# Modulation units moved between the halves of a weight split, spread over more phases, and combined in five parts

## The chip, the cores and the metric

The kernel runs on one core of a Trainium2 chip. The metric is the device time of one execution in microseconds (us). The engines are TensorE (PE, matrix products), VectorE (DVE), ScalarE (ACT), GpSimd (POOL) and SyncE (SP, which issues most of the DMA transfers). Each works through its own instructions in order and waits for semaphores that the others raise.

## The reference: two pairs of layers on 256 tokens of width 1024

The first block has two layers, each a token mixer (latent attention with twelve heads, then sliding-window attention with ALiBi and sinks), cross attention to 256 memory rows, an output projection, and a squared-relu MLP of width 4096. The second block has an even layer (short convolution and a gated linear recurrence) and an odd layer (stick-breaking attention with 16 heads), each with a SwiGLU network of width 2816. Its two layers are modulated by a vector c:

```python
def ada_modulation(c, ada_w, ada_b):
    m = jax.nn.silu(c) @ ada_w + ada_b
    return jnp.split(m, N_MOD, axis=-1)
...
    sh_m, sc_m, g_m, sh_f, sc_f, g_f = ada_modulation(c, ada_w, ada_b)
    h = modulate(rms_norm(x, mix_norm), sh_m, sc_m)
...
    x = x + g_m[:, None, :] * y
    hf = modulate(rms_norm(x, ffn_norm), sh_f, sc_f)
    return x + g_f[:, None, :] * swiglu(hf, ffn_w_gate, ffn_w_up, ffn_w_down)
```

ada_w is 1024 x 6144 per layer, c a single row of 1024. So per layer six vectors of 1024 numbers are needed: shift, scale and gate of the mixer, and the same of the network. The product does not depend on x; it can be worked out any time before the second block wants it.

## The kernel before

**The weight stream.** All large weights pass through rings of two slots of 2 MB each, in the order w_in, mem0, w_uq, w_ukv, mem1, w_o0 (2 slots), up0 (8), down0 (8), swa (4), w_o1 (2), up1 (8), down1 (8), lru_in (5), lru_out (2), gate_up0 (11), ffn_down0 (8), qkv (6), sb_out (2), gate_up1 (11), ffn_down1 (8). Products are made of two numbers of reduced precision per value. SP loads a slot into raw in two transfers; ScalarE's split (L738) copies it to w_hi in two halves, for which it waits until TensorE is through with the slot two before; VectorE's split (L1255) makes w_lo = raw - w_hi, also in two halves, each as soon as that half of w_hi is there. TensorE's two_bank_slot (L2234) waits for both halves of w_lo and then does 2 banks x 2 blocks x 8 chunks x 3 products = 96 matmuls of 256 columns (L2172 to L2174). A slot of ffn_down has 66.

**What stands around a split on VectorE.** In an up slot, hidden (L1812) makes a_lo of bank 0 and of bank 1 (L1819), each after ScalarE has taken that bank (relu and square, L1007 to L1012), and then the split of the slot after next. In a down slot there is only the split, with add_to_residual at j=3. In gate_up, hidden (L2029) multiplies gate by up (L2038), makes a_lo (L2040) and splits. In ffn_down a turn (L2068) is split, add (the product, gated, goes to x, L2053), split.

**The modulation.** The 2 x 6144 outputs are 24 groups of 512 (12 per layer), each of 4 quarters of the 1024 inputs: 96 *units*. A unit needs 512 KB of ada_w, which the POOL queue loads (L571) into one of two buffers; load m waits until unit m - 2 has been worked off. On VectorE a unit is two operations of 128x512 (L1761, the first of a group is L1758). After four units ada_group_done (L1774) transposes the sums (L1779) and reduces them (L1782) into ada_part. When a layer's 12 groups are there, ada_combine on TensorE (L2222) adds the four quadrants with four small matmuls into the norm bank's second half, and modulation on VectorE (L1785) adds the bias and makes the gains.

**Where the units stand before.** Always two at a time, by phase: w_o0 4 units, up0 16, down0 16, swa 4, w_o1 4, up1 16, down1 16, gate_up0 20. In up they stand between the two a_lo of a slot, in down ahead of the split, in gate_up0 ahead of the multiply, in w_o behind the add (the second pair), in swa behind the split. So every unit stands ahead of the split of its slot or behind it, never inside. Layer 0's combination is in the middle of up1 (behind four slots), layer 1's in ffn_down0 behind its first turn. The loops over slots are hardware loops on VectorE in mlp, gate_up and ffn_down.

## Time and profile before

| | us |
|---|---|
| median of three runs | 1190.78 (1190.17 to 1193.43) |
| the profiled execution | 1182.13 |
| its span | 1180.5 |
| TensorE busy | 1156.9 (98%) |
| VectorE busy | 881.7 (75%) |
| ScalarE busy | 634.3 (54%) |
| granted TensorE clock, mean | 1.00 of full speed |

Times in the views count from the start of the span. In a row of the timeline, what stands in brackets is how long the engine was idle before the row and which instruction of which engine released it; "x4" is a run of four instructions of one kind, and the duration is that of the run.

### The profile page before, as it was taken

What the parts mean: (1) busy time and instruction counts of PE and PEld (TensorE: products, weight loads), DVE (VectorE), ACT (ScalarE), POOL (GpSimd) and SP (SyncE); (2) the same over time, 40 slices, a digit from 0 to 9 for tenths busy, and PEclk for the clock granted to TensorE, in tenths of its full rate; (3) what the DMA queues carried; (4) which work ended last, traced back from release to release, by engine and by line L of the source; (5) the groups of instructions that cost most, each with busy time, mean ns of one, the idle gap of its engine ahead of it and who ended that gap; (6) DMA issues with size and microseconds to landing.
All of it is one profiled execution on the core that took longest, in us unless ns stands there. A gap on an engine that the chain in (4) does not pass through costs nothing.

```text
span 1180.5 us, 23101 instructions
## 1 busy us (share of the span) xinstructions
PE 1156.9 (98%) x9525; PEld 1119.7 (95%) x9525; DVE 881.7 (75%) x1174; ACT 634.3 (54%) x853; POOL 95.6 (8%) x147
## 2 busy tenths in 40 slices
PE   8999999999989999999999999999999999999998
PEld 8999999999988999999999999999988879999998
DVE  5876898878876798888998888887576557855543
ACT  7558566633347567634468463443455574634332
POOL 0000011111124011111200001010000000000000
PEclk9999999999999999999999999999999999999999
DMA  9352588887772488788844657877645504565462
GB/s 329 138 179 73 190 292 272 312 308 235 263 267 72 157 275 305 273 302 294 306 167 143 198 159 253 281 265 240 207 165 172 199 1 143 186 206 180 146 196 85
DMA packets 150060, 248.97 MB, mean 211 GB/s; under 512 B 5553, under 2 KB 80922, under 8 KB 149978
## 3 DMA queue, kind: packets, MB, share of 16 engines
q1 hardware_dynamic: 135858, 197.17, 49.6%
q0 software_dynamic: 13952, 50.60, 11.8%
q8 instruction: 60, 0.98, 0.4%
q14 instruction: 22, 0.18, 0.0%
q10 hardware_dynamic: 168, 0.04, 0.0%
HBM read 246.74 MB, written 1.05 MB: 210 GB/s over the span
## 4 chain that ended last, share of the span: by engine, by line
PE 67%; DVE 17%; ACT 4%; issue 3%; DMA 3%; POOL 0%; DVEq 0%; POOLq 0%; ACTq 0%
PE ps L2172 19%; PE ps L2173 19%; PE ps L2174 19%; DVE w_lo L1260 7%; DVE scratch L1761 4%; DMA ada_raw<-in_l_ada_w 3%; ACT w_hi L745 2%; PE ps L2454 2%; PE ps L2320 1%; PE ps L2764 1%; PE ps L2436 1%; DVE ps L1779 1%; ACT h_both L812 1%; PE ps L2738 1%; PE ps L2423 1%
## 5 line engine op out<-in xcount | busy, mean ns | idle before, releaser
L1260 DVE TENSOR_TENSOR w_lo<-raw,w_hi 128x2048 fp32r<-128x2048 f32 (+4 forms) x196 | 412.7, 2144 | 88.4 <-ACT w_hi L745 87.9
L745 ACT ACTIVATE w_hi<-raw 128x2048 fp32r<-128x2048 f32 (+4 forms) x196 | 342.2, 1791 | 156.4 <-PE ps L2174 151.9
L2172 PE MATMUL ps<-h_both,w_hi 128*128 128x256 f32 (+1 forms) x1296 | 360.6, 278 | 7.9 <-DVE w_lo L1260 4.4
L2173 PE MATMUL ps<-h_both,w_hi 128*128 128x256 f32 (+1 forms) x1296 | 358.8, 277 | 0.0
L2174 PE MATMUL ps<-h_both,w_lo 128*128 128x256 f32 (+1 forms) x1296 | 358.7, 277 | 0.0
L2172 PEld LDWEIGHTS ps<-h_both,w_hi 128*128 128x128 f32 (+1 forms) x1296 | 242.7, 187 | 9.9 <-issue 5.0
L2173 PEld LDWEIGHTS ps<-h_both,w_hi 128*128 128x128 f32 (+1 forms) x1296 | 243.4, 188 | 0.1
L2174 PEld LDWEIGHTS ps<-h_both,w_lo 128*128 128x128 f32 (+1 forms) x1296 | 242.7, 187 | 0.0
L2172 PE MATMUL ps<-a_both,w_hi 128*128 128x256 f32 x864 | 238.8, 276 | 0.6 <-DVE xT L2053 0.6
L2173 PE MATMUL ps<-a_both,w_hi 128*128 128x256 f32 x864 | 238.5, 276 | 0.0
L2174 PE MATMUL ps<-a_both,w_lo 128*128 128x256 f32 x864 | 238.5, 276 | 0.0
L2172 PEld LDWEIGHTS ps<-a_both,w_hi 128*128 128x128 f32 x864 | 162.2, 188 | 0.8 <-DVE xT L2053 0.8
L2173 PEld LDWEIGHTS ps<-a_both,w_hi 128*128 128x128 f32 x864 | 162.2, 188 | 0.0
L2174 PEld LDWEIGHTS ps<-a_both,w_lo 128*128 128x128 f32 x864 | 162.2, 188 | 0.0
L1761 DVE SCALAR_TENSOR_TENSOR scratch<-ada_raw,silu_c,scratch 128x512 f32<-128x512 f32 x168 | 126.2, 751 | 13.6 <-DMA ada_raw<-in_l_ada_w 6.1
L571 POOL DMA_DIRECT2D ada_raw<-in_l_ada_w x96 | 69.5, 724 | 623.6 <-DVE scratch L1761 623.3
L1153 ACT ACTIVATE a_both<-a_full 128x512 fp32r<-128x512 f32 x18 | 11.4, 633 | 107.5 <-DVE a_full L2038 107.5
L1007 ACT ACTIVATE a_full<-ps 128x512 f32<-128x512 f32 x32 | 19.0, 595 | 51.2 <-PE ps L2174 51.1
L2172 PE MATMUL ps<-h_wide,w_hi 128*128 128x258 f32 x160 | 45.8, 286 | 0.2 <-DVE xT L1441 0.2
L2173 PE MATMUL ps<-h_wide,w_hi 128*128 128x258 f32 x160 | 45.4, 284 | 0.0
L2174 PE MATMUL ps<-h_wide,w_lo 128*128 128x258 f32 x160 | 45.3, 283 | 0.0
L2172 PE MATMUL ps<-w_hi,h_both 128*128 128x512 f32 (+1 forms) x112 | 42.8, 382 | 0.7 <-issue 0.7
(423 smaller groups left out, 1806.6 us busy)
## 6 DMA issues: line engine op xcount, KB each, us to landing
ada_raw<-in_l_ada_w POOLq DMA_DIRECT2D x96, 512.0 KB, 6.9
raw<-in_mlp_w_up SPq DMA_DIRECT2D x32, 1024.0 KB, 6.4
raw<-in_mlp_w_down SPq DMA_DIRECT2D x32, 1024.0 KB, 6.9
raw<-in_l_ffn_w_gate SPq DMA_DIRECT2D x22, 1024.0 KB, 5.4
raw<-in_l_ffn_w_up SPq DMA_DIRECT2D x22, 1024.0 KB, 8.6
raw<-in_l_ffn_w_down SPq DMA_DIRECT2D x16, 768.0 KB, 6.0
raw<-in_l_w_qkv SPq DMA_DIRECT2D x12, 1024.0 KB, 6.9
raw<-in_l_w_in SPq DMA_DIRECT2D x10, 1024.0 KB, 6.3
```

The lines of the kernel that those rows point to most:

```text
L571: pool.dma_start(ada_raw[:, slot, :, :], ada[l][:, 2 * quarter:2 * quarter + 2, group])\
L745: nc.scalar.activation(w_hi[:, s.slot, cut], raw[:, s.slot, cut], ACT.Copy).then_inc(split_hi, 1)
L812: ins = nc.scalar.activation(h_hi[:, ch, :], xT[:, ch, :], ACT.Copy, scale=col_a[:, gain_at + ch:gain_at + ch + 1])
L1007: nc.scalar.activation(full, acc(b if j else FIRST_UP_BANKS[b]).rearrange("p (c t) -> p c t", c=2), ACT.Relu)\
L1260: nc.vector.tensor_tensor(w_lo[:, s.slot, cut], raw[:, s.slot, cut], w_hi[:, s.slot, cut].bitcast(F32), ALU.subtract).then_inc(split_lo, 1)
L1761: ins = nc.vector.scalar_tensor_tensor(ada_sum, w, c, ada_sum, ALU.mult, ALU.add)
L1779: nc.vector.transpose(ps[:, ADA_BANK, :], ada_sum).then_inc(ada_turned, 1)
L2172: nc.tensor.matmul(to, sh, mh, start=first, stop=False, skip_group_check=True)
L2173: nc.tensor.matmul(to, sh, ml, start=False, stop=False, skip_group_check=True)
L2174: return nc.tensor.matmul(to, sl, mh, start=False, stop=last, skip_group_check=True)
L2320: ins = nc.tensor.transpose(ps[0:ncols, bank, ch * T + t * P:ch * T + (t + 1) * P], src(ch, t), ident[:, :])
L2454: ins = nc.tensor.matmul(ps[:, 6 + g % 2, qt * T + j * HD:qt * T + (j + 1) * HD], p[:, n * P:(n + 1) * P], v, start=j == 0 and n == 0, sto ...
```

## The change

One counter now runs over the units, and a call asks for the next n of them. Where they stand:

- w_o0 2, up0 14 (1, 1 and then 2 per slot), down0 14 (not in its last slot), swa 2, w_o1 2, up1 12 (1, 1, 1, 2, 2, 2, 1, 2), down1 14, gate_up0 18, ffn_down0 6, qkv 4, gate_up1 8.
- In up, down and gate_up they stand between the two halves of the split; in ffn_down0 ahead of a turn's first split; in qkv, w_o and swa behind a split.
- The combination and modulation come in five parts of 8, 4, 6, 4 and 2 groups: behind up1, in lru_in behind slot 1, in ffn_down0 behind the first turn, in sb_out behind slot 0, and ahead of ffn_down1.
- VectorE's loops over slots are written out. POOL issues the same 96 loads, in other portions around its work on masks.

```diff
+MOD_PARTS = ((0, 8, 0), (8, 12, 1), (12, 18, 0), (18, 22, 1), (22, 24, None))
+UP_UNITS = ((1, 1, 2, 2, 2, 2, 2, 2), (1, 1, 1, 2, 2, 2, 1, 2))
...
+            def ada_units(n):
+
+                for m in range(ada_begun[0], ada_begun[0] + n):
+                    ada_unit(m)
+                    if m % 4 == 3:
+                        ada_group_done(m // 4)
+                ada_begun[0] += n
...
+            def modulation(k):
+
+                first, last, which = MOD_PARTS[k]
+                l, at, n = first // ADA_GROUPS, 4 * (first % ADA_GROUPS), 4 * (last - first)
+                c = COL_B[f"ada_b{l}"] + at
+                dve.wait_ge(ada_combined, k + 1)
+                nc.vector.tensor_tensor(mod[:, l, at:at + n], ps[:, NORM_BANK, T:T + n], col_b[:, c:c + n], ALU.add).then_inc(mod_kept, 1)
+                dve.wait_ge(mod_kept, k + 1)
+                if which is not None:
+                    key = ("mix", "ffn")[which] + str(l)
+                    link(nc.vector.scalar_tensor_tensor(modg[:, l, which, :], mod[:, l, 8 + 24 * which:16 + 24 * which], 1.0,
+                                                        col_a[:, COL_A[key]:COL_A[key] + KD], ALU.add, ALU.mult))
...
             split(Slot("w_o0", 1))
-            ada_units("w_o0", 0)
+            ada_units(2)
             add_to_residual("w_o0", 0, following="mlp0")
             split(Slot("w_o0", 2))
             add_to_residual("w_o0", 1, following="mlp0")
-            ada_units("w_o0", 1)
...
+                def hidden(j):
...
+                    split(Slot(f"up{l}", j + 2), (0,))
+                    ada_units(UP_UNITS[l][j])
+                    split(Slot(f"up{l}", j + 2), (1,))
...
-                for j in range(8):
+                for j in range(7):
...
-                    ada_units(f"down{l}", j)
                     following = ("attn1", "final")[l]
                     if j == 3:
                         add_to_residual(f"down{l}", 0, following, pairs=(0,))
-                    if j < 7:
-                        split(Slot(f"down{l}", j + 2))
+                    split(Slot(f"down{l}", j + 2), (0,))
+                    ada_units(2)
+                    split(Slot(f"down{l}", j + 2), (1,))
...
             split(Slot("swa", 3))
-            ada_units("swa", 1)
             wait_part(Slot("swa", 2), 0)
...
-            ada_units("w_o1", 1)
             mlp(1)
...
             split(Slot("lru_in", 3))
+            modulation(1)
...
-                    split(ahead)
+                    split(ahead, (0,))
+                    if j < 10 or l == 0:
+                        ada_units(2 - l)
+                    split(ahead, (1,))
...
+                for i in range(3):
+                    if l == 0:
+                        ada_units(2)
+                    split(Slot(f"ffn_down{l}", 2 * i + 2))
+                    add(i)
+                    split(Slot(f"ffn_down{l}", 2 * i + 3))
+                    if l == 0 and i == 0:
+                        modulation(2)
...
                     split(Slot("qkv", j + 2))
+                if 1 <= j < 5:
+                    ada_units(1)
...
             split(Slot("sb_out", 1))
+            modulation(3)
             add_gated("sb_out", 0, 1, "ffn1")
...
+            def ada_combine(k):
+
+
+                first, last, _ = MOD_PARTS[k]
+                pe.wait_ge(ada_summed, last)
+                if k:
+                    pe.wait_ge(mod_kept, k)
...
             as_chunks_arrive("sb_out", 3)
+            ada_combine(3)
             two_bank_slot("sb_out", 1)
```

How the instructions stand at three places, on VectorE and once on TensorE. (The line numbers of the changed kernel differ a little: its w_lo is L1262, its units L1761 and L1764, its transpose and reduction L1780 and L1782, the gated adds L1466 and L2045, the combining matmuls L2219.)

VectorE in up0, from the split of one slot to the split of the next (a_both is a_lo, the rows of L1761 and L1764 are two units that end a group), before:

```order
L1260 TENSOR_TENSOR w_lo<-raw,w_hi 128x2048 [waits split_hi] x2
L1819 TENSOR_TENSOR a_both<-a_full,a_both 128x512 [waits hid_hi]
L1761 SCALAR_TENSOR_TENSOR scratch<-ada_raw,silu_c,scratch 128x512 [waits ada_step,ada_loaded0]
L1761 SCALAR_TENSOR_TENSOR scratch<-ada_raw,silu_c,scratch 128x512 [waits ada_step]
L1761 SCALAR_TENSOR_TENSOR scratch<-ada_raw,silu_c,scratch 128x512 [waits ada_step,ada_loaded1]
L1761 SCALAR_TENSOR_TENSOR scratch<-ada_raw,silu_c,scratch 128x512 [waits ada_step]
L1779 STREAM_TRANSPOSE ps<-scratch 128x512 [waits ada_step]
L1782 TENSOR_REDUCE ada_part<-ps 128x16 [waits ada_turned]
L1819 TENSOR_TENSOR a_both<-a_full,a_both 128x512 [waits hid_hi]
L1260 TENSOR_TENSOR w_lo<-raw,w_hi 128x2048 [waits split_hi] x2
```

and with the change:

```order
L1262 TENSOR_TENSOR w_lo<-raw,w_hi 128x2048 [waits split_hi]
L1819 TENSOR_TENSOR a_both<-a_full,a_both 128x512 [waits hid_hi] x2
L1262 TENSOR_TENSOR w_lo<-raw,w_hi 128x2048 [waits split_hi]
L1764 SCALAR_TENSOR_TENSOR scratch<-ada_raw,silu_c,scratch 128x512 [waits ada_step,ada_loaded0]
L1764 SCALAR_TENSOR_TENSOR scratch<-ada_raw,silu_c,scratch 128x512 [waits ada_step]
L1764 SCALAR_TENSOR_TENSOR scratch<-ada_raw,silu_c,scratch 128x512 [waits ada_step,ada_loaded1]
L1764 SCALAR_TENSOR_TENSOR scratch<-ada_raw,silu_c,scratch 128x512 [waits ada_step]
L1780 STREAM_TRANSPOSE ps<-scratch 128x512 [waits ada_step]
L1782 TENSOR_REDUCE ada_part<-ps 128x16 [waits ada_turned]
L1262 TENSOR_TENSOR w_lo<-raw,w_hi 128x2048 [waits split_hi]
```

The units, their transpose and reduction stood behind the a_lo of bank 0 and ahead of that of bank 1, and so ahead of the whole split; now they stand behind both a_lo and behind the first half of the split, and only its second half follows them. At the mouth of up0, where a pair and its group's end stood between h_both and the split of slot 1, nothing stands now.

VectorE at the end of gate_up0 and the first turn of ffn_down0, before (a_full and a_both are the multiply and a_lo of the last gate_up slot, the first w_lo is ffn_down0's slot 1, the second its slot 2, xT the add of the turn):

```order
L2038 TENSOR_TENSOR a_full<-a_full,ps 128x512 [waits acc_out0,parts_done]
L2040 TENSOR_TENSOR a_both<-a_full,a_both 128x512 [waits hid_hi]
L1260 TENSOR_TENSOR w_lo<-raw,w_hi 128x1408 [waits split_hi] x2
L1761 SCALAR_TENSOR_TENSOR scratch<-ada_raw,silu_c,scratch 128x512 [waits ada_step,ada_loaded0]
L1761 SCALAR_TENSOR_TENSOR scratch<-ada_raw,silu_c,scratch 128x512 [waits ada_step]
L1761 SCALAR_TENSOR_TENSOR scratch<-ada_raw,silu_c,scratch 128x512 [waits ada_step,ada_loaded1]
L1761 SCALAR_TENSOR_TENSOR scratch<-ada_raw,silu_c,scratch 128x512 [waits ada_step]
L1779 STREAM_TRANSPOSE ps<-scratch 128x512 [waits ada_step]
L1782 TENSOR_REDUCE ada_part<-ps 128x16 [waits ada_turned]
L1260 TENSOR_TENSOR w_lo<-raw,w_hi 128x1408 [waits split_hi] x2
L2053 SCALAR_TENSOR_TENSOR xT<-ps,mod,xT 128x256 [waits parts_done] x2
```

and with the change:

```order
L1764 SCALAR_TENSOR_TENSOR scratch<-ada_raw,silu_c,scratch 128x512 [waits ada_step]
L1764 SCALAR_TENSOR_TENSOR scratch<-ada_raw,silu_c,scratch 128x512 [waits ada_step,ada_loaded1]
L1764 SCALAR_TENSOR_TENSOR scratch<-ada_raw,silu_c,scratch 128x512 [waits ada_step]
L1262 TENSOR_TENSOR w_lo<-raw,w_hi 128x1408 [waits split_hi]
L1764 SCALAR_TENSOR_TENSOR scratch<-ada_raw,silu_c,scratch 128x512 [waits ada_step,ada_loaded0]
L1764 SCALAR_TENSOR_TENSOR scratch<-ada_raw,silu_c,scratch 128x512 [waits ada_step]
L1764 SCALAR_TENSOR_TENSOR scratch<-ada_raw,silu_c,scratch 128x512 [waits ada_step,ada_loaded1]
L1764 SCALAR_TENSOR_TENSOR scratch<-ada_raw,silu_c,scratch 128x512 [waits ada_step]
L1780 STREAM_TRANSPOSE ps<-scratch 128x512 [waits ada_step]
L1782 TENSOR_REDUCE ada_part<-ps 128x16 [waits ada_turned]
L1262 TENSOR_TENSOR w_lo<-raw,w_hi 128x1408 [waits split_hi] x2
L2045 SCALAR_TENSOR_TENSOR xT<-ps,mod,xT 128x256 [waits parts_done] x2
```

Here the first three L1764 rows are of the pair of the last gate_up slot, which now stands inside the split of ffn_down0's slot 1; the next pair follows behind a single half of w_lo, where before a whole split, and with it the wait for w_hi, stood between two pairs.

VectorE at sb_out, before (h_both is the attention's output, xT the gated add of slot 0, bank by bank):

```order
L1747 TENSOR_TENSOR h_both<-ps,h_both 128x512 [waits mix_hi] x2
L1260 TENSOR_TENSOR w_lo<-raw,w_hi 128x2048 [waits split_hi] x2
L1464 SCALAR_TENSOR_TENSOR xT<-ps,mod,xT 128x256 [waits parts_done]
L1464 SCALAR_TENSOR_TENSOR xT<-ps,mod,xT 128x256
L1464 SCALAR_TENSOR_TENSOR xT<-ps,mod,xT 128x256 [waits parts_done]
L1464 SCALAR_TENSOR_TENSOR xT<-ps,mod,xT 128x256
```

and with the change:

```order
L1749 TENSOR_TENSOR h_both<-ps,h_both 128x512 [waits mix_hi] x2
L1262 TENSOR_TENSOR w_lo<-raw,w_hi 128x2048 [waits split_hi] x2
L1791 TENSOR_TENSOR mod<-ps,col_b 128x16 [waits ada_combined]
L1795 SCALAR_TENSOR_TENSOR modg<-mod,col_a 128x8 [waits mod_kept]
L1466 SCALAR_TENSOR_TENSOR xT<-ps,mod,xT 128x256 [waits parts_done,dve_step]
L1466 SCALAR_TENSOR_TENSOR xT<-ps,mod,xT 128x256
L1466 SCALAR_TENSOR_TENSOR xT<-ps,mod,xT 128x256 [waits parts_done]
L1466 SCALAR_TENSOR_TENSOR xT<-ps,mod,xT 128x256
```

The two operations of modulation(3) have come in ahead of the first gated add, with a wait for TensorE's combination. On TensorE that stands between the two slots of sb_out:

```order
L2160 MATMUL ps<-h_both,w_hi 128x256
L2161 MATMUL ps<-h_both,w_lo 128x256
L2219 MATMUL ps<-ada_part,line_h 32x16 [waits mod_kept,ada_summed]
L2219 MATMUL ps<-ada_part,line_h 32x16 x3
L2159 MATMUL ps<-h_both,w_hi 128x256 [waits acc_out0,split_lo]
L2160 MATMUL ps<-h_both,w_hi 128x256
```

The matmul behind it, the first of slot 1, waits for acc_out0, the add of bank 0, and for w_lo.

## Rows read from the trace of the kernel before

**Rows 1.** Page, busy time per engine, and TensorE's granted clock in 40 slices.
```profile
PE 1156.9 (98%) x9525; PEld 1119.7 (95%) x9525; DVE 881.7 (75%) x1174; ACT 634.3 (54%) x853; POOL 95.6 (8%) x147
...
PEclk9999999999999999999999999999999999999999
```

**Rows 2.** TensorE's waits over the whole span: us in total, times, longest.
```profile
PE ps L2172 <- DVE w_lo L1260: 4.4, 3, 2.0
...
PE ps L2422 <- DVE qx L1890: 3.3, 1, 3.3
...
PE ps L2172 <- DVE xT L1441: 1.8, 2, 1.7
```

**Rows 3.** Timeline of VectorE at the mouth of up0: start, us, line, tiles, [idle before].
```profile
142.50 3.18 DVE L1761 SCALAR_TENSOR_TENSOR scratch<-ada_raw,silu_c,scratch 128x512 f32<-128x512 f32 x4
...
147.08 4.48 DVE L1260 TENSOR_TENSOR w_lo<-raw,w_hi 128x2048 fp32r<-128x2048 f32 x2
```

**Rows 4.** Timeline of TensorE, same place.
```profile
151.61 0.39 PE L2172 MATMUL ps<-h_both,w_hi 128*128 128x256 f32 x1 [1.96 <-DVE w_lo L1260]
```

**Rows 5.** Timelines at the head of swa: VectorE, then TensorE.
```profile
343.49 3.22 DVE L1761 SCALAR_TENSOR_TENSOR scratch<-ada_raw,silu_c,scratch 128x512 f32<-128x512 f32 x4 [2.42 <-DMA ada_raw<-in_l_ada_w]
...
350.25 0.34 PE L2422 MATMUL ps<-swa_kT,swa_qT 64*128 64x128 f32 x1 [3.34 <-DVE qx L1890]
```

**Rows 6.** Timeline of ScalarE in up0.
```profile
195.92 0.60 ACT L1007 ACTIVATE a_full<-ps 128x512 f32<-128x512 f32 x1 [3.51 <-PE ps L2174]
...
206.80 0.60 ACT L1007 ACTIVATE a_full<-ps 128x512 f32<-128x512 f32 x1 [3.51 <-PE ps L2174]
```

**Rows 7.** Timeline of VectorE in up0.
```profile
193.83 0.48 DVE L1758 TENSOR_SCALAR scratch<-ada_raw,silu_c 128x512 f32<-128x512 f32 x1
...
199.69 4.49 DVE L1260 TENSOR_TENSOR w_lo<-raw,w_hi 128x2048 fp32r<-128x2048 f32 x2 [0.89 <-ACT w_hi L745]
```

**Rows 8.** Timeline of down0: ScalarE, then VectorE.
```profile
239.50 3.73 ACT L745 ACTIVATE w_hi<-raw 128x2048 fp32r<-128x2048 f32 x2 [5.40 <-PE ps L2174]
...
241.46 4.49 DVE L1260 TENSOR_TENSOR w_lo<-raw,w_hi 128x2048 fp32r<-128x2048 f32 x2 [1.56 <-ACT w_hi L745]
```

**Rows 9.** Timeline of VectorE in gate_up1, slots without units.
```profile
1039.29 0.69 DVE L2038 TENSOR_TENSOR a_full<-a_full,ps 128x512 f32 x1 [3.19 <-PE ps L2174]
...
1042.48 4.50 DVE L1260 TENSOR_TENSOR w_lo<-raw,w_hi 128x2048 fp32r<-128x2048 f32 x2 [1.00 <-ACT w_hi L745]
```

**Rows 10.** Timeline around ffn_down0's first turn: VectorE, then ScalarE.
```profile
804.89 3.16 DVE L1260 TENSOR_TENSOR w_lo<-raw,w_hi 128x1408 fp32r<-128x1408 f32 x2 [0.58 <-ACT w_hi L745]
...
808.56 3.21 DVE L1761 SCALAR_TENSOR_TENSOR scratch<-ada_raw,silu_c,scratch 128x512 f32<-128x512 f32 x4 [0.50 <-DMA ada_raw<-in_l_ada_w]
...
820.46 0.20 DVE L1789 TENSOR_TENSOR mod<-ps,col_b 128x48 f32<-128x48 f32 x1
...
824.58 2.65 ACT L745 ACTIVATE w_hi<-raw 128x1408 fp32r<-128x1408 f32 x2 [5.95 <-PE ps L2174]
...
832.06 1.38 ACT L745 ACTIVATE w_hi<-raw 128x1408 fp32r<-128x1408 f32 x1 [4.83 <-PE ps L2174]
```

**Rows 11.** Line L571, the modulation loads' issues, over the whole span.
```profile
DMA to landing us min/median/max: 4.0/6.9/9.0
```

**Rows 12.** Timeline of TensorE at the first combination, in up1.
```profile
454.60 0.28 PE L2174 MATMUL ps<-h_both,w_lo 128*128 128x256 f32 x1
...
455.09 0.39 PE L2172 MATMUL ps<-h_both,w_hi 128*128 128x256 f32 x1
```

**Rows 13.** Timeline at sb_out: VectorE, then TensorE.
```profile
979.73 0.87 DVE L1464 SCALAR_TENSOR_TENSOR xT<-ps,mod,xT 128x256 f32<-128x256 f32 x2 [2.76 <-PE ps L2174]
...
980.88 0.28 PE L2172 MATMUL ps<-h_both,w_hi 128*128 128x256 f32 x1
```

**Rows 14.** Window behind swa's stop: length, busy us of each engine, PEclk, DMA share, GB/s.
```profile
352.00:366.00 14.00, 13.01 (x111) 11.31 (x109) 7.05 (x28) 10.53 (x35) 9.01 (x6) 1.00 0.01 2
```

**Rows 15.** Timeline of VectorE in qkv, one of four reductions.
```profile
892.23 0.69 DVE L2116 TENSOR_REDUCE sb_ms<-sb_sq 128x8 f32<-128x512 f32 x1 [2.58 <-ACT sb_sq L1186]
```

More of the change, by code:

```diff
@@ L125 @@
 ADA_GROUPS = 12
-ADA_SLOTS = ADA_GROUPS + 1
-ADA_GROUP = {"w_o0": 0, "up0": 1, "down0": 5, "swa": 9, "w_o1": 10, "up1": 11, "down1": 15, "gate_up0": 19}
+MOD_PARTS = ((0, 8, 0), (8, 12, 1), (12, 18, 0), (18, 22, 1), (22, 24, None))
+UP_UNITS = ((1, 1, 2, 2, 2, 2, 2, 2), (1, 1, 1, 2, 2, 2, 1, 2))
 HIDDEN_BEFORE = {"0": 0, "1": 16, "ffn0": 32, "ffn1": 43}
@@ L1750, in _, with ada_unit @@
             ada_sum = scratch[:, 2:4, :].rearrange("p c t -> p (c t)")
-            def ada_unit(m, slot, quarter, loads):
-                dve.wait_ge(ada_loaded[slot], loads)
+            def ada_unit(m):
+                slot, quarter = m % 2, m % 4
+                dve.wait_ge(ada_loaded[slot], 16 * (m // 2 + 1))
                 for q in range(2):
@@ L1762, in ada_unit @@
                     ins.then_inc(ada_step, 1)
-            def ada_units(phase, j, i=None):
-                slot_no = 2 * ADA_GROUP[phase] + j
-                grow = (lambda per, first: first) if i is None else (lambda per, first: i * per + first)
-                for u in range(2):
-                    ada_unit(grow(4, 2 * slot_no + u), u, 2 * (j % 2) + u, grow(32, 16 * (slot_no + 1)))
-                if j % 2:
-                    layer = ADA_GROUP[phase] > ADA_GROUP["w_o1"] if i is not None else slot_no // 2 >= ADA_GROUPS
-                    ada_group_done(grow(1, slot_no // 2 + 1), ADA_SLOTS if layer else 0)
@@ L1785, in modulation @@
[L1785 to L1793 removed]
+            ada_begun = [0]
@@ L1829, in mlp @@
                 link(nc.vector.tensor_tensor(r_squared, r_squared, r_squared, ALU.mult))
-                hidden(1)
-                if l:
-                    dve.wait_ge(ada_combined, 1)
-                with dve.Fori(2, 4) as i:
-                    hidden(i)
-                for j in range(8):
+                for j in range(2, 8):
+                    hidden(j)
+                for j in range(7):
                     if l and j == 1:
@@ L2061, in ffn @@
                 split(Slot(f"gate_up{l}", 3))
-                with dve.Fori(1, 4) as i:
-                    for j in range(2):
-                        hidden(j, i)
-                for j in (8, 9, 10):
+                for j in range(2, 11):
                     hidden(j)
-                def turns(first):
-                    with dve.Fori(first, 3) as i:
-                        split(Slot(f"ffn_down{l}", 2, i, 2))
-                        add(i)
-                        split(Slot(f"ffn_down{l}", 3, i, 2))
-                if l == 0:
-                    ada_units("gate_up0", 9)
-                    split(Slot("ffn_down0", 2))
-                    add(0)
-                    split(Slot("ffn_down0", 3))
-                    modulation(1)
-                    turns(1)
-                else:
-                    turns(0)
+                if l:
+                    modulation(4)
+                for i in range(3):
+                    if l == 0:
+                        ada_units(2)
+                    split(Slot(f"ffn_down{l}", 2 * i + 2))
[3 more added lines that the diff above has]
+                        modulation(2)
                 if l == 0:
```

111 lines of the change are left out of this document (45 added, 66 removed).

## The prediction

> **What bounds the kernel now.** I read the busy line first: TensorE is busy 1156.9 of 1180.5 us, VectorE 881.7, and the granted clock stays in the top tenth throughout [rows 1]. So the time is TensorE's own work plus the stops in it, and a change of VectorE's order can only matter where it makes or removes such a stop. The list of TensorE's waits then names them: 4.4 us on w_lo, 3.3 us on qx, 1.8 us on xT, the rest shorter [rows 2]. The timeline shows what stood ahead of VectorE in each. At the start of up0 two modulation units (3.18 us), the transpose and the reduction of their group run from 142.50 to 147.08, only then the split of up0's slot 1 (4.48 us), and TensorE waits 1.96 us for it [rows 3, 4]. At the head of swa TensorE's scores wait 3.34 us for VectorE, which waited 2.42 us for a unit's load and then did 3.22 us of units and their transpose and reduction, all ahead of swa_kT and qx [rows 5].
>
> Next, how much room a split has. In up0 ScalarE takes bank 1 of a slot at 195.92 and of the next at 206.80, so a slot lasts P = 10.88 us [rows 6]. Call E the slot's end, some 0.2 us before that row (195.72). w_lo of the slot after next waits for its w_hi, starts at E + 3.97 and ends at E + 8.46 [rows 7]; it is needed at E + 10.88. **Slack: 2.4 us.** The units of before run ahead of it, from 193.83 for some 2.9 us [rows 7], while VectorE would wait for TensorE anyway: they are free. In the down stage w_hi starts with TensorE's last matmul, at 239.50 (E + 0.2), and w_lo ends at 245.95, E + 6.65 [rows 8]: slack 4.2. For gate_up the slots of layer 1, which carry no units, show it: the multiply starts at 1039.29 (about E + 0.4) and w_lo ends at 1046.98 [rows 9], so E + 8.1: slack 2.8.
>
> **The change, part by part.**
>
> *Units between the halves.* Now the first half of w_lo starts where it did, since it waits for w_hi; the units follow, and the second half after them. TensorE waits for both halves, so the units' full length goes behind the point that was the late one. A unit is 2 operations, a pair of units 3.18 us [rows 3]; a group's first operation takes 0.48 [rows 7], so a pair with it takes 2.9; a pair that ends a group takes 4.58 with transpose and reduction (142.50 to 147.08 [rows 3], so 1.4 for these two); one unit that ends a group 3.0. Against the slack: a stall of max(0, insert - slack - stall of the slot before), since a stalled slot gives the next one that much more room.
>
> - up0 (inserts from slot 3 on: 3.0, 2.9, 4.58, 2.9, 4.58, 2.9, 4.58). 4.58 - 2.4 = 2.15 on every second slot, nothing or half a us on the others, as the stall before covers them: slots 5, 7 and slot 1 of down0 give 3 x 2.15 (slots 4 and 5 share theirs). Slot 3 has the variance of the delayed norm behind its split, on which the relu and the next banks wait: 2.1. Sum 8.55, and 0.1 at each of five restarts, as the first matmul behind a stop takes 0.39 us [rows 4] where one takes 0.28 elsewhere [rows 13]: 9.0.
> - down0: 4.58 - 4.2 = 0.4 at j=1; at j=3 and 4 add_to_residual (two pairs of 0.7 us operations) shares VectorE: 1.25 each. Sum 2.9.
> - Removed at the mouth of mlp0: the stop of [rows 4], 2.1 (1.96 and its restart). Removed at the end of down0, where j=7's pair and its group's end stood ahead of the final add: TensorE's 1.7 us wait on xT [rows 2] and its restart, 1.8, and 0.26 of a short wait behind it. Net to the head of swa: 9.0 + 2.9 - 2.1 - 2.06 = +7.7; with small waits on the relu +8.2.
> - swa: the units ahead of swa_kT are gone, so swa_kT starts as soon as its bank is full: **-3.4**, the stop of 3.34 [rows 5].
> - up1 and down1: single units make inserts smaller: slot 3 again 2.1, then 0.75, 0.9 and 0.55, and down1's four group ends 0.4 each; 5.9, restarts 0.5, less the same stop at the mouth, 2.1: **+4.3**.
> - gate_up0: a pair with a first operation 2.9 against 2.8, nothing; group ends 4.58: about 1.3, 1.6, 1.6 for slots 5, 7, 9. The splits of ffn_down0 are shorter (3.16 a pair [rows 10]) but so are its slots (7.48 by ScalarE's two rows of the same group), and the pair in its slot 1 costs 1.35. Sum 5.9.
> - ffn_down0's first turn: units 78 and 79 use the buffers of 76 and 77, so their loads go out only when those are done. Before, a pair stood ahead of its multiply, 5 us sooner, and even so the last pair waited 0.50 us for its load at 808.56 [rows 10]. Now 76 and 77 run between the halves of the split, with only a half split behind them. With the 6.9 us median from a load's issue to its landing [rows 11] the units end 17.3 us after the last gate_up slot, the split behind them at 20.4, and the add, which frees the bank, at 20.9, where TensorE wants it at 16.3: a stop of 4.5, against some 0.8 now, combination included. I take +3.7; with the shortest and longest landing of the same row, 4.0 and 9.0 us, it is 0.8 to 5.8. With -0.8 for small waits in gate_up0 that the new stops swallow, the stage is **+8.8**.
>
> *Five combinations in place of two.* One costs about 0.5: from 454.60 to 455.09 the slot's matmuls stand still for 0.49 where one follows another by 0.11 (10.88 over 96), and the first one behind takes 0.1 longer [rows 12]. Three more: **+1.5**. Nothing excludes that they are free where TensorE waits anyway, so 0.5 to 1.5.
>
> *Modulation(3) at sb_out* is put ahead of add_gated(0). Today that add runs at 979.73, while TensorE does block 1, and frees bank 0 for slot 1, which starts at 980.88 without a stop [rows 13]. Now it waits until block 1 and the combination are through (981.4); then come the two short operations of modulation (0.2 us each, as in ffn_down0 [rows 10]), the add of 0.87 and some 0.1 from each to the next: slot 1 starts at about 983.0. Of the 2.15, 0.5 is counted above: **+1.65**. Queued behind it on VectorE are the second add and the next split, needed 10.9 us later.
>
> *Free.* The four qkv units (1.6, the last 3.0) stand where VectorE idles 2.58 us or more ahead of a reduction [rows 15]; gate_up1 carries one unit (1.6, or 3.0 with a group's end) against 2.8; modulation in lru_in and ffn_down0 has no one waiting. If that cover is missing, each such unit costs up to its length less the slack, 0.2, eight times: under 2 us. The unrolled loops save VectorE branches off the path: 0. The POOL queue issues the same 96 loads, in other portions around its mask work: 0, except where named.
>
> Sum: 8.2 - 3.4 + 4.3 + 8.8 + 1.5 + 1.65 = **+21.0** on the profiled execution's 1182.13, thus 1203.1. The median of the three timed runs, 1190.78, stands 8.65 above that execution; the stops should be the same there, so I forecast 1190.8 + 21.0 = **1211.8 us**. 0.3% (3.6 us) is about what a measurement of this kernel can tell from no change.
>
> **The rivals.**
> - *Loads between the halves.* VectorE waits 6.1 us for modulation loads today, all but the swa one unseen by TensorE. In their new place every such wait is in front of a half split. That adds up to 6: 1218. For: POOL holds a load until the buffer is free, so a unit's load has about one slot of time. Against: median landing 6.9 is under a slot's 10.88 [rows 6, 11]. Chance 0.10.
> - *The clock falls after a stop.* The stop of 4.5 us in ffn_down0 is longer than the longest of today behind the first loads, 3.34 us in swa, behind which the granted clock still reads 1.00 [rows 5, 14]. If it fell to the lower of its two levels, 1.2 in place of 2.4 GHz, one ffn_down slot of 7.48 us [rows 10] would take twice as long: +7.5, 1219. The Trainium skill (TensorE: Matmul & The Clock Gate, HAM oscillation) says that a wait between bursts of matmuls lets the array start the next burst at the lower clock, each time; by that rule swa should already show it, and the trace does not agree. Chance 0.05.
> - *Only the group ends stall*, and those by half, because the first half starts earlier than I read: of the stalls in the list (9.0 + 2.9 + 6.4 + 5.9 + 3.7 = 27.9) half comes: about 1198. Chance 0.07.
> - *The other side: faster.* The mechanism is the cover. If VectorE's insert stays under the slack (2.4 us in up, 4.2 in down) no split is late; the removed stops (2.1 + 2.06 + 3.4 + 2.1 = 9.7) stand against 3.15 for combinations and sb_out: 1184. It decides at an insert of 2.4 us in up. For: single units (1.6) stay below. Against: most inserts are 2.9 and more, and the first half cannot start earlier than w_hi lets it. Chance 0.05; that the two just cancel, 0.03.
> - *The change does not do what it says*: excluded, VectorE's order shows the units between the halves.
>
> **How the numbers follow.** Main case 0.70 (1203 to 1220, from its terms' bounds: the load in ffn_down0 -2.8 to +2.2, the add_to_residual pairs, slot 3 and the combinations about as much again), loads 0.10, clock 0.05, group ends only 0.07, faster 0.05, same 0.03. The range 1200 to 1221 leaves out the faster and same cases, most of the group-end case and the tails. Slower 0.92, same 0.03, faster 0.05.
>
> **What would show it.** In the changed profile: TensorE's waits on w_lo rise from 4.4 us to over 20, in stops of about 2 us on alternate slots of up0; the 3.34 us on qx is gone; a stop of over 3 us on xT at the first turn of ffn_down0; one of about 2 us on xT at sb_out's slot 1; five sets of combining matmuls. It is wrong if w_lo's second half ends ahead of the last matmul of the slot before it in up0, if stops on w_lo total less than 10 us, or if the first half of w_lo starts well before E + 3.9.

## The result, and the profile after

The changed kernel takes **1225.86 us** (median of four runs, 1225.70 to 1227.43) against 1191.88 for the one before in the same comparison: a ratio of **1.0293, 95% interval 1.0266 to 1.0321**, slower by 34 us. I had forecast slower, 1211.8 us, with 1221 as the upper end. The sign was right and the size was not: 34 us in place of 21.

The page of the changed kernel, busy times and TensorE's granted clock, and under it TensorE's waits over the whole span (us in total, times, longest):

```profile
PE 1192.1 (97%) x9549; PEld 1152.8 (94%) x9549; DVE 883.4 (72%) x1177; ACT 635.2 (52%) x853; POOL 98.2 (8%) x147
...
PEclk9999999999999999999999999998999999999999
```

```profile
PE ps L2159 <- DVE w_lo L1262: 11.4, 13, 2.1
PE ps L2159 <- DVE xT L2045: 4.3, 1, 4.3
...
PE ps L2159 <- ACT a_full L1009: 2.1, 2, 1.1
...
PE ps L2159 <- DVE xT L1466: 1.5, 1, 1.5
```

Against [rows 1] TensorE is busy 35.2 us longer (1192.1 for 1156.9), with the same products and 24 small matmuls more; it idles only 8.4 us longer (span 1224.1 less 1192.1, against 1180.5 less 1156.9). Against [rows 2] the waits of the forecast are all there: w_lo 11.4 us in 13 stops for 4.4 in 3; the 3.3 us on qx and the 1.8 on xT L1441 are gone; 4.3 us on xT in ffn_down0, 1.5 at sb_out. So the profile says at once where my sum is short: **not in the stops, but in the matmuls themselves**, which I had taken to keep their pace; the stops come to less than I had summed. The profiled execution of before was a quick one of its kind (1182.13 where the timed runs of all comparisons take 1186 to 1200), so part of the 35 us is owed to that; the experiments separate the rest.

The stop in ffn_down0, VectorE and then TensorE:

```profile
839.86 1.54 DVE L1764 SCALAR_TENSOR_TENSOR scratch<-ada_raw,silu_c,scratch 128x512 f32<-128x512 f32 x2 [2.37 <-DMA ada_raw<-in_l_ada_w]
843.37 1.54 DVE L1764 SCALAR_TENSOR_TENSOR scratch<-ada_raw,silu_c,scratch 128x512 f32<-128x512 f32 x2 [1.98 <-DMA ada_raw<-in_l_ada_w]
...
846.32 3.15 DVE L1262 TENSOR_TENSOR w_lo<-raw,w_hi 128x1408 fp32r<-128x1408 f32 x2
849.38 0.87 DVE L2045 SCALAR_TENSOR_TENSOR xT<-ps,mod,xT 128x256 f32<-128x256 f32 x2
```

```profile
845.30 0.28 PE L2219 MATMUL ps<-ada_part,line_h 128*32 128x24 f32 x8
849.92 0.58 PE L2159 MATMUL ps<-a_both,w_hi 128*128 128x256 f32 x1 [4.35 <-DVE xT L2045]
850.30 0.42 PE L2160 MATMUL ps<-a_both,w_hi 128*128 128x256 f32 x1
850.51 0.41 PE L2161 MATMUL ps<-a_both,w_lo 128*128 128x256 f32 x1
```

Units 78 and 79 wait 2.37 and 1.98 us for their loads, the split and the add come behind them, and TensorE stands for 4.35 us. What follows it was not in my main case: the matmuls behind the stop take 0.41 us by the trace and follow each other by 0.21, half the pace. The windows show the granted clock there and behind the stop at the mouth of down0 (columns as in [rows 14]):

```profile
246.00:254.00 8.00, 5.88 (x38) 5.71 (x38) 7.73 (x8) 3.71 (x2) 0.72 (x1) 0.79 0.73 221
254.00:262.00 8.00, 8.00 (x69) 8.00 (x69) 3.24 (x3) 0.00 (x0) 1.45 (x2) 1.00 0.96 364
844.00:856.00 12.00, 7.65 (x54) 7.41 (x53) 11.65 (x16) 2.64 (x2) 1.12 (x2) 0.72 0.80 264
```

0.79 over 8 us and 0.72 over 12 us would be some 5 us, but the second fall begins inside the stop, where nothing runs: 15 and 21 matmuls follow each other by 0.21 us, some 4 us lost (an estimate: 36 times 0.1). The rest of the slower matmuls has no clock that explains it.

### The profile page after: what moved, and what is told of

Its sections match the earlier page's. It is cut to its first block, busy times and chain, and to the rows that moved or that the text cites. A ratio compares the mean times of both kernels' runs of the same rounds, so it can differ in the third digit from the quotient of the medians.

```text
span 1224.1 us, 22908 instructions
## 1 busy us (share of the span) xinstructions
PE 1192.1 (97%) x9549; PEld 1152.8 (94%) x9549; DVE 883.4 (72%) x1177; ACT 635.2 (52%) x853; POOL 98.2 (8%) x147
## 4 chain that ended last, share of the span: by engine, by line
PE 76%; DVE 10%; issue 4%; ACT 3%; DMA 1%; POOL 0%; DVEq 0%; ACTq 0%; POOLq 0%
PE ps L2159 23%; PE ps L2161 22%; PE ps L2160 22%; DVE w_lo L1262 4%; DVE scratch L1764 3%; ACT w_hi L747 2%; PE ps L2443 2%; PE ps L2309 1%; PE ps L2756 1%; PE ps L2425 1%; DVE ps L1780 1%; PE ps L2730 1%; DMA ada_raw<-in_l_ada_w 1%; PE ps L2412 1%; PE ps L2772 1%
## 5 line engine op out<-in xcount | busy, mean ns | idle before, releaser
L1262 DVE TENSOR_TENSOR w_lo<-raw,w_hi 128x2048 fp32r<-128x2048 f32 (+4 forms) x196 | 416.7, 2144 | 109.7 <-ACT w_hi L747 109.4
L2159 PE MATMUL ps<-h_both,w_hi 128*128 128x256 f32 (+1 forms) x1296 | 368.9, 285 | 11.0 <-DVE w_lo L1262 6.2
L2160 PE MATMUL ps<-h_both,w_hi 128*128 128x256 f32 (+1 forms) x1296 | 366.6, 283 | 0.0
L2161 PE MATMUL ps<-h_both,w_lo 128*128 128x256 f32 (+1 forms) x1296 | 366.5, 283 | 0.0
L2159 PEld LDWEIGHTS ps<-h_both,w_hi 128*128 128x128 f32 (+1 forms) x1296 | 247.8, 191 | 14.1 <-issue 11.2
L2159 PE MATMUL ps<-a_both,w_hi 128*128 128x256 f32 x864 | 243.0, 281 | 9.2 <-DVE w_lo L1262 4.8
L2160 PEld LDWEIGHTS ps<-h_both,w_hi 128*128 128x128 f32 (+1 forms) x1296 | 247.9, 191 | 0.1
L2161 PEld LDWEIGHTS ps<-h_both,w_lo 128*128 128x128 f32 (+1 forms) x1296 | 247.9, 191 | 0.1
L2160 PE MATMUL ps<-a_both,w_hi 128*128 128x256 f32 x864 | 241.9, 280 | 0.0
L2161 PE MATMUL ps<-a_both,w_lo 128*128 128x256 f32 x864 | 241.8, 280 | 0.0
L2159 PEld LDWEIGHTS ps<-a_both,w_hi 128*128 128x128 f32 x864 | 164.8, 191 | 10.6 <-issue 5.7
L2160 PEld LDWEIGHTS ps<-a_both,w_hi 128*128 128x128 f32 x864 | 164.0, 190 | 0.0
L571 POOL DMA_DIRECT2D ada_raw<-in_l_ada_w x96 | 69.2, 721 | 919.3 <-DVE scratch L1764 919.0
L1764 DVE SCALAR_TENSOR_TENSOR scratch<-ada_raw,silu_c,scratch 128x512 f32<-128x512 f32 x168 | 126.1, 750 | 11.6 <-DMA ada_raw<-in_l_ada_w 4.3
L1155 ACT ACTIVATE a_both<-a_full 128x512 fp32r<-128x512 f32 x18 | 11.4, 632 | 104.3 <-DVE a_full L2032 104.3
L1819 DVE TENSOR_TENSOR a_both<-a_full,a_both 128x512 fp32r<-128x512 f32 x32 | 22.1, 689 | 30.9 <-ACT a_both L1014 30.7
```

The costliest lines, as they stand in the source:

```text
L571: pool.dma_start(ada_raw[:, slot, :, :], ada[l][:, 2 * quarter:2 * quarter + 2, group])\
L1262: nc.vector.tensor_tensor(w_lo[:, s.slot, cut], raw[:, s.slot, cut], w_hi[:, s.slot, cut].bitcast(F32), ALU.subtract).then_inc(split_lo, 1)
L1764: ins = nc.vector.scalar_tensor_tensor(ada_sum, w, c, ada_sum, ALU.mult, ALU.add)
L1819: nc.vector.tensor_tensor(a_lo[:, at_pair, :], a_full[:, at_pair, :], a_hi[:, at_pair, :].bitcast(F32), ALU.subtract).then_inc(hid_lo, 1)
L2159: nc.tensor.matmul(to, sh, mh, start=first, stop=False, skip_group_check=True)
L2160: nc.tensor.matmul(to, sh, ml, start=False, stop=False, skip_group_check=True)
```

## The experiments

I looked at the spacing, how long after one matmul of 256 columns the next begins. It is 0.113 us nearly everywhere before (10.88 us for 96, [rows 6]; short stretches and the first half of gate_up0 run at 0.118); in the changed kernel it is 0.120 in up0, up1 and both gate_up, and 0.118 in most of down0 and a part of down1. A count of matmuls in 20 us of down0 (they read a_both) and of gate_up1 (they read h_both) shows it well, and each experiment below is read with it. Before, first profile:

```profile
256.00:276.00 20.00, 20.00 (x179) 20.00 (x178) 14.81 (x18) 6.08 (x6) 2.90 (x4) 1.00 0.79 282
1080.00:1100.00 20.00, 20.00 (x179) 20.00 (x178) 10.59 (x8) 9.69 (x8) 0.00 (x0) 1.00 0.56 177
```

179 in both. The changed kernel:

```profile
256.00:276.00 20.00, 20.00 (x171) 19.87 (x170) 10.10 (x9) 5.19 (x3) 1.90 (x3) 1.00 0.70 249
1080.00:1100.00 20.00, 20.00 (x169) 20.00 (x168) 13.20 (x10) 8.22 (x7) 1.42 (x2) 1.00 0.70 225
```

**Before, unchanged, and the units ahead of the split.** `before_again` is the kernel before, profiled once more. `after_units_ahead` is the changed kernel with:

```diff
+                        if b == 0:
+                            ada_units(UP_UNITS[l][j])
-                    split(Slot(f"up{l}", j + 2), (0,))
-                    ada_units(UP_UNITS[l][j])
-                    split(Slot(f"up{l}", j + 2), (1,))
+                    split(Slot(f"up{l}", j + 2))
```

and likewise ahead of the split in down and ahead of the multiply in gate_up.

> The kernel before, unchanged, profiled once more. Three theories stand against each other on why TensorE's matmuls of 256 columns follow each other by 0.113 us nearly everywhere before and by 0.118 to 0.120 us in most stages of the changed kernel. RESTART (a stop of TensorE, or a wait that ends just in time, sets the spacing of the matmuls until the next such event): 0.113 in up0, down0, up1 and down1 again, time within 10 us of 1191. EXECUTION (the spacing is a state of one loading of the program, whatever the kernel): other stages than in the first profile are at 0.118 to 0.120, and the time follows, 1182 to 1210. CODE (the spacing belongs to TensorE's own program): 0.113 in the same stages as in the first profile.

Measured 1196.18 us, clock 0.994, TensorE busy 1169.2. The spacing was 0.113 in the same stages as before, except gate_up1 and most of ffn_down1, which ran at 0.118 (172 in the same 20 us of gate_up1). So two values, 0.113 and 0.118, occur at the same place of the same program, but no 0.120. And three of before's four longer stops, all without effect on the clock in the first profile, are followed by a lower clock here, in the same program. The stop at the end of down0 was also twice as long here, 3.5 us for 1.7. First two windows of the first profile (the third is [rows 14]), then before_again:

```profile
314.00:322.00 8.00, 6.34 (x54) 6.17 (x54) 6.01 (x11) 4.88 (x7) 0.74 (x2) 1.00 0.67 223
420.00:428.00 8.00, 6.51 (x57) 6.51 (x58) 7.79 (x10) 6.24 (x8) 1.45 (x2) 1.00 0.70 241
```

```profile
PE ps L2172 <- DVE xT L1441: 3.7, 2, 3.5
...
314.00:322.00 8.00, 4.50 (x32) 4.34 (x31) 6.71 (x12) 2.21 (x4) 1.44 (x2) 0.85 0.97 295
352.00:362.00 10.00, 7.91 (x43) 7.29 (x44) 2.83 (x12) 6.72 (x12) 5.51 (x7) 0.66 0.33 122
428.00:434.00 6.00, 5.75 (x36) 5.75 (x37) 5.79 (x10) 4.29 (x4) 1.44 (x2) 0.72 0.79 255
...
1080.00:1100.00 20.00, 20.00 (x172) 20.00 (x172) 10.51 (x8) 9.68 (x8) 0.00 (x0) 1.00 0.66 209
```

> The changed kernel with its units moved back ahead of the whole split in up, down and gate_up; the rest of the change stays. COVER (the units' place makes the stops): TensorE's waits on w_lo fall from 11.4 us to about 2, the clock no longer falls at the mouth of down0. RESTART: with the stops goes the spacing of 0.118 to 0.120 us in up and down, 113 ns returns there, and the time falls by 11 + 15 to 20 us, to 1195 to 1200. CODE: the spacing stays at 0.118 to 0.120, time about 1212 to 1215. EXECUTION: no forecast for the spacing; the time falls by the stops alone on average, to 1213.

Measured **1195.24 us** (ten runs, 1194.48 to 1195.55), ratio 1.0011 (0.9988 to 1.0035) to before. COVER holds for the stops: of the waits on w_lo none is left in up, down and gate_up, the clock is 1.00 throughout, and 30.6 us are back. But the spacing in up and gate_up stayed at 0.120 with no stop anywhere near, so RESTART falls as the cause of it:

```profile
256.00:276.00 20.00, 20.00 (x179) 20.00 (x178) 15.02 (x13) 6.54 (x4) 2.17 (x3) 1.00 0.77 280
1080.00:1100.00 20.00, 20.00 (x169) 20.00 (x168) 12.12 (x10) 9.68 (x8) 0.90 (x2) 1.00 0.78 258
```

down0 is at 0.113 here, gate_up1 at 0.120: what reads h_both is slow, what reads a_both is not.

**Only the units moved, in the program of before.** `before_units_between`:

```diff
-                            if b == 0:
-                                ada_units(f"up{l}", j, i)
-                        split(Slot(f"up{l}", j + 2, i, 2))
+                        split(Slot(f"up{l}", j + 2, i, 2), (0,))
+                        ada_units(f"up{l}", j, i)
+                        split(Slot(f"up{l}", j + 2, i, 2), (1,))
```

and the same in down and gate_up0.

> The kernel before with only the units moved between the halves of the split in up, down and gate_up0; TensorE's program is word for word that of before. COVER: stops of 2 us on alternate up slots and 0.4 to 1.3 in down and gate_up0, in all 20 to 27 us of stops if the matmuls keep 0.113 us, 10 to 15 if they go to 0.120 (a slower slot gives VectorE 0.65 us more). RESTART: spacing 0.118 to 0.120 us from the first of these stops on, time 1191 + 30 to 40. CODE: spacing 0.113 throughout, as this is before's program, time 1191 + 20 to 27. EXECUTION: spacing as in before_again.

Measured **1245.98 us**, ratio 1.0433 (1.0384 to 1.0483), 52 us above before: more than any theory said. The stops are those of COVER:

```profile
PE ps L2175 <- DVE w_lo L1260: 25.2, 17, 2.2
PE ps L2175 <- DVE xT L1441: 11.5, 2, 5.9
PE ps L2175 <- ACT a_full L1007: 6.7, 2, 3.4
```

w_lo rises by 21 us to 25.2; with the full two units per slot the add at the end of down waits as well. The spacing is 0.113 in nearly all of up0, most of up1 and all of gate_up1: a stop need not change it. But 0.118 holds for two fifths of down0 and of down1, which run at 0.113 in both profiles of before, and for three quarters of gate_up0 (before: a bit over half), so RESTART is not excluded for this value. And the clock is at 0.985 over the whole span, the lowest of all kernels here: it fell behind nine of the stops. Against the first profile of before TensorE idles 39 us more and is busy 25 us longer, so stops cost more than their own length.

`before_one_stop`, one stop made by hand in down0 by doing half a split three times more:

> The kernel before with one stop made by hand: in down0, behind the first half of w_lo of slot 4, the same operation is done three more times (6.9 us) before the second half. The slack there is 4.2 us, so TensorE should stop once, for about 2.6 us, and there is no other change. COVER alone: the stop and nothing else, +2.6 us. RESTART: the spacing behind it goes to 0.118 or 0.120 us up to the next stop at the head of swa, some 480 matmuls at 5 to 7 ns, so +2.6 and 2 to 3.5 more. CLOCK: the granted clock falls for a few us behind the stop, and 20 to 30 matmuls take 0.21 us, +2 to 3 more. CODE and EXECUTION: spacing behind the stop as ahead of it.

The time is inconclusive: 1196.91 us (1192.5 to 1207.5), ratio 1.003 (0.9998 to 1.0063); the spread of before, 1187.8 to 1199.3 in this comparison, covers it. The trace says more. VectorE's delay made two stops, 2.9 us and, one slot on, 2.2:

```profile
277.32 0.36 PE L2181 MATMUL ps<-a_both,w_hi 128*128 128x256 f32 x1 [2.92 <-DVE w_lo L1260]
277.52 0.28 PE L2182 MATMUL ps<-a_both,w_hi 128*128 128x256 f32 x1
277.64 0.28 PE L2183 MATMUL ps<-a_both,w_lo 128*128 128x256 f32 x1
...
291.09 0.36 PE L2181 MATMUL ps<-a_both,w_hi 128*128 128x256 f32 x1 [2.23 <-DVE w_lo L1260]
```

The clock did not fall behind either, though it fell behind three of before's own stops of 2 to 3 us in this execution. The 47 matmuls behind the first and some 90 behind the second follow each other by 0.118, those between and later in the stage by 0.113, as in all of down0 in both profiles of before. That speaks for RESTART where 0.118 is concerned, in one execution.

**The address of h_both.** The change also widens a small tile, line_h, from 48 to 64 numbers and cuts ada_part from 13 to 12 groups; these lines are not in the diff shown above, and my sum had nothing for them. line_h is declared ahead of h_both, ada_part behind it: h_both moves up by 64 bytes in each partition, from 131392 (64 above a multiple of 128) to 131456 (a multiple of 128), and the arena with a_both stays (64 above one). The weight rings begin at a multiple of 128 in both kernels. Three kernels test this:

```diff
 before_h_moved (on before)
+        final_gain = sb("final_gain", [P, KD])
+        silu_c = sb("silu_c", [P, KD])
         h_wide = sb("h_wide", [P, 2, KD, T + 2], F32R)
 after_h_back (on the changed kernel), after_ahead_h_back (on after_units_ahead)
-        line_h = sb("line_h", [P, 64])
+        line_h = sb("line_h", [P, 48])
...
+        sb("line_g", [P, 16])
         ada_part = sb("ada_part", [P, ADA_GROUPS, 16])
```

(In the first, the two tiles' declarations further down go.)

> The kernel before with two small tiles, final_gain and silu_c (8 numbers each per partition), declared ahead of h_wide. That moves h_both up by 64 bytes in each partition, to where the changed kernel has it (131456 in place of 131392), and leaves every instruction and the arena with a_both in place. ADDRESS (the matmuls that read h_both follow each other by 0.120 us at the one address and by 0.113 at the other): spacing 0.120 us in up0, up1, gate_up0 and gate_up1, 0.113 still in down0, down1 and ffn_down; some 3860 matmuls at 6.7 ns, 26 us, less the stops that the slower slots swallow: 1194 + 20 to 26. CODE (the spacing belongs to TensorE's program): 0.113, time as before, 1194.

Measured 1203.90 us, ratio **1.0107** (1.0078 to 1.0137), with no instruction added, taken out or moved:

```profile
256.00:276.00 20.00, 20.00 (x179) 20.00 (x179) 14.34 (x13) 7.41 (x4) 2.10 (x4) 1.00 0.81 279
1080.00:1100.00 20.00, 20.00 (x169) 20.00 (x168) 11.75 (x8) 9.68 (x8) 0.00 (x0) 1.00 0.60 189
```

ADDRESS holds, CODE falls: 169 in gate_up1, 179 in down0. The loss is 13 us, less than the 20 to 26 expected, since some stops shrink (w_lo 2.7 us for 4.4 [rows 2]) and probably since other executions of before are at 0.118 here and there, as in before_again, which is 4.5 of the 6.7 ns.

> The changed kernel with line_h cut from 64 to 48 numbers and a spacer of 16 ahead of ada_part: h_both lies where it lay before, everything behind the spacer stays. ADDRESS: spacing 0.113 in up and gate_up; the matmuls win 26 us, but the slack of a split in up falls from 3.1 us to 2.4, so the stops of the up and gate_up slots grow towards what I forecast from a spacing of 0.113: time 1194 + 15 to 22. CODE: no difference to the changed kernel, 1226.

Measured 1219.17 us, ratio 1.0234 (1.0198 to 1.0269), 28.5 us above before: better than the changed kernel by 6.7 only. As expected the slack fell and the stops grew, w_lo from 11.4 us to 15.9 (rows below); but the spacing was 0.118 in half of up0 and up1 and in all of down1 and gate_up1, so the difference to before came out some 6 us above the 15 to 22 that I gave.

```profile
PE 1179.4 (97%) x9549; PEld 1139.5 (94%) x9549; DVE 883.5 (73%) x1177; ACT 635.4 (52%) x853; POOL 98.2 (8%) x147
```

```profile
PE ps L2160 <- DVE w_lo L1263: 15.9, 13, 2.3
PE ps L2160 <- DVE xT L2046: 4.2, 1, 4.2
...
PE ps L2160 <- ACT a_full L1010: 2.9, 2, 1.7
...
PE ps L2160 <- DVE xT L1467: 1.5, 1, 1.5
```

> The changed kernel with the units ahead of the whole split (as in after_units_ahead, 1195.2 us) and h_both back at its old address. ADDRESS: the 26 us of spacing go and nothing comes in their place, as no split is late: 1168 to 1175, faster than both kernels. CODE: 1195.

Measured 1174.5 to 1183.4 us in five runs, median 1176.1 (a sixth took 2337.5, twice the others, and is left out); ratio **0.9893** (0.9850 to 0.9936): faster than both kernels. The profiled execution has 0.118 in places too: in two thirds of gate_up0, behind the wait of 0.9 us below, and in sb_out, behind none.

```profile
PE 1158.9 (99%) x9549; PEld 1122.1 (96%) x9549; DVE 882.4 (75%) x1177; ACT 633.8 (54%) x853; POOL 98.2 (8%) x147
```

```profile
256.00:276.00 20.00, 20.00 (x179) 20.00 (x178) 13.86 (x17) 7.81 (x7) 2.89 (x4) 1.00 0.88 315
1080.00:1100.00 20.00, 20.00 (x179) 20.00 (x178) 15.36 (x14) 7.94 (x8) 0.00 (x0) 1.00 0.51 173
```

```profile
PE ps L2158 <- DVE xT L1467: 1.5, 1, 1.5
PE ps L2158 <- DVE w_lo L1263: 0.9, 1, 0.9
```

Together (medians, us):

| | h_both 64 above a multiple of 128 | at a multiple of 128 |
|---|---|---|
| before | 1190.7 to 1194.5 | 1203.9 |
| changed, units ahead | 1176.1 | 1195.2 |
| changed, units between | 1219.2 | 1225.9 |

The units' place costs 43 us at the one address and 31 at the other; the address costs 19, 13 or 7. The two do not simply add up: a slower slot leaves VectorE more time, at 0.120 the slack of an up slot is 0.64 us larger, and the 0.118 of some stages takes part of what the better address gives.

**Which address it is.** `after_ahead_h_96` has line_h at 56 numbers, so that h_both begins 96 above a multiple of 128; `after_ahead_w_moved` leaves h_both at a multiple of 128 and puts 64 bytes ahead of the weight rings instead.

> As after_ahead_h_back, but with line_h of 56 numbers: h_both begins at 131424, which is 96 above a multiple of 128, where the kernel before has 64 and the changed one 0. ADDRESS, if it is the place within 128 bytes that counts: another spacing than 0.120, 0.113 if any odd start serves, in between if the rows are cut by the start. CODE: as in after_units_ahead, 0.120.

One execution: 1194.09 us, spacing of h_both's matmuls 0.118 (171 in the 20 us of gate_up1) in every stage that reads it, which is so in no profile with h_both at 64: hardly better than the changed kernel's place. That any start off a multiple of 128 serves is thereby as good as excluded. The number alone would not do: down0 ran at 0.118 here too (172), with a_both where it was and no stop near.

> after_units_ahead with a spacer of 64 bytes ahead of the weight rings and line_h back to 48 numbers: h_both stays where the changed kernel has it (131456, a multiple of 128), a_both stays where it was (64 above one), but raw, w_hi and w_lo now begin 64 above a multiple of 128 in place of at one. ADDRESS ALONE (where the moving operand begins): h_both's matmuls still follow each other by 0.120 us and a_both's by 0.113, as in after_units_ahead, time 1195. ADDRESS BESIDE THE WEIGHTS (the place of the moving operand against that of the weights): the two change sides, h_both's go to 0.113 and a_both's to 0.120; 26 us less on some 3860 matmuls, 17 more on 2590, time about 1186 to 1190.

One execution: 1191.51 us, and the two changed sides:

```profile
256.00:276.00 20.00, 20.00 (x171) 20.00 (x170) 14.79 (x15) 4.37 (x4) 2.89 (x4) 1.00 0.75 261
1080.00:1100.00 20.00, 20.00 (x179) 20.00 (x179) 13.51 (x12) 8.39 (x7) 0.71 (x1) 1.00 0.71 232
```

171 in down0, 179 in gate_up1, with h_both and a_both where they were. So it is the place of the moving operand **against that of the weights**, not its own. Over the whole span a_both's matmuls follow each other by 0.1187 us here (0.1134 in after_units_ahead), h_both's by 0.1142 (0.1199).

**The combination at sb_out.** `ahead_h_back_sb` is after_ahead_h_back with ada_combine(3) moved ahead of the stick-breaking loop, and modulation(3) behind its first softplus.

> after_ahead_h_back with the fourth combination moved from between sb_out's two slots to the end of qkv, and its modulation behind the first softplus, so that the gated add of sb_out's slot 0 waits for nothing but its product. My forecast gave this place 1.65 us plus 0.5 for the combination. If that is right the stop of 1.5 us at sb_out's slot 1 goes and no other comes: 1.5 to 2 us below after_ahead_h_back (1174.5 to 1183.4), so 1173 to 1181. If the combination at its new place holds up the stick-breaking products, as much comes back there.

Measured 1179.79 us (six runs, 1175.06 to 1181.83), ratio 0.9880 (0.9835 to 0.9925). The 1.5 us on xT L1467 is gone from the waits and nothing new stands in the list, but the time is not below after_ahead_h_back's, whose own spread of 9 us is larger than the term. In the profiles the two differ by where 0.118 stands: gate_up1 and most of ffn_down1 here, sb_out there, neither behind a stop of 1 us or more. The run shows the wait, not its worth.

## Why the prediction was right and wrong

**The places and sizes of the stops: right.** In after_h_back, where the spacing is the 0.113 that I reckoned with, TensorE's waits by stretch stand beside my terms. From 160 to 238 us (up0, two rows), 238 to 325 (down0) and 700 to 834 (gate_up0):

```profile
PE ps L2160 <- DVE w_lo L1263: 3.5, 3, 1.7
PE ps L2160 <- ACT a_full L1010: 1.7, 1, 1.7
...
PE ps L2160 <- DVE w_lo L1263: 5.8, 4, 2.3
...
PE ps L2160 <- DVE w_lo L1263: 5.5, 4, 1.6
```

Up0 and down0 11.0 us for 11.45; gate_up0 5.5 for 5.9; from the list further up, ffn_down0 4.2 for 4.5 and sb_out 1.5 for 1.65 and 0.5. Only up1 and down1 were too dear, 2.3 for 5.9: single units fit better than I reckoned. What a combination costs by itself, my 0.5, no run separates. Also right: the stops removed at the mouths of the MLPs, at the end of down0 and in swa do not come back. Taken together, after_ahead_h_back, which has those removals and no units between halves, is 14.6 us below before (1190.69 in the same comparison), where my terms made it 6.5 (9.7 of removals less 3.15 for combinations and sb_out).

**The step that failed: P = 10.88 us.** I took the spacing of the matmuls as a constant and summed stops only. The runs show three parts of it that I left out.
- *The address.* The widened line_h was read as a detail. It puts h_both at the same place within 128 bytes as the weights, 0.120 for 0.113 us on some 3860 matmuls: 7 us in this kernel, after the stops that the wider spacing swallows (w_lo waits 11.4 us with it and 15.9 without; the rest to the 20 that I named as a sign is up1 and down1), 13 in the program of before, and 19 where the units make no stop.
- *The pace of the matmuls in the better place.* From after_ahead_h_back to after_h_back the only edit is the units' place. The waits of the four rows above grow by 22.1 us, but TensorE's busy time grows by 20.5 (1158.9 to 1179.4): the durations of a_both's and h_both's matmuls, which overlap, add up to 18.8 more, and by their starts they take some 16 us more. The lower clock accounts for about 4 of that, 40 matmuls at 0.21; the rest is spacing of 0.118. Some of its stretches start at a stop (at 199.5, 477.5 and 829.6 us), but the longest do not: down1 from 512 us on, and gate_up1 with ffn_down1, some 6 us, which ran so in before_again and ahead_h_back_sb too, without any unit between halves. So the profile does not show how much of it the stops bring. The times of all runs lie at least 31 us apart (1214.6 and more against 1183.4 and less), of which waits and clock make 26; what remains is slower spacing, whatever sets it. I had 0.1 us per restart.
- *The clock.* My rival had it at 0.05 because before's longest stop was followed by a clock of 1.00 [rows 14]. That was one execution. In before_again three of its four stops, this one among them, are followed by 0.66 to 0.85, and in the changed kernel both stops of over 2 us by a lower clock. The Trainium skill's rule (TensorE: Matmul & The Clock Gate, HAM oscillation), that waits between bursts of matmuls start the next burst at the lower clock, holds here for many stops and not for all. In no profile without stops of about 2 us or more between its matmuls did the clock fall. These falls may also explain part of why 1182.13 and 1190.78 stand apart: I put the 8.65 us down as an offset, but the timed runs of before in the later comparisons have a mean clock of 0.992 to 0.999, where that profile has 1.000; each 0.001 is at most 1.2 us by estimate.

So the sum reads, in medians: I had 27.9 us for the units between the halves, less 6.9 for all the rest (the 6.5 above and small waits), 21 together. Measured are 43.0 for the first (1219.17 less 1176.13: 22 in stops, 20 in slower matmuls), less 14.6 for the rest, plus 6.7 for the address: 35, from 1190.69 to 1225.86. That the removed stops were worth more than I gave them has probably the same reason as that the new ones cost more: the clock is 0.994 to 0.999 in before's runs of that comparison and 0.999 or more in after_ahead_h_back's.

**The rivals.** "Loads between the halves" came true in ffn_down0 alone, where I had it in the main case. "Only the group ends" is excluded: after_h_back's stops come to 23.0 us, where that rival has 14. "Faster" needed inserts under the slack; after_ahead_h_back, where the units stand ahead of the split, shows what that is worth at the old address.

What stays open: what sets 0.113 or 0.118 in a stage of one execution, a restart or something else, and why the clock falls behind one stop of 2 us and not behind the next. No run here tells that apart.
